# Hybrid decoder trunk: the chunk inverse in two halves, the K and R projections as one block

## What is computed

```python
def step(S, inp):
    r_t, w_t, k_t, v_t, kk_t, a_t = inp
    sa = jnp.einsum('bhvk,bhk->bhv', S, kk_t)
    S = (S * w_t[:, :, None, :] - sa[..., None] * (kk_t * a_t)[:, :, None, :]
         + v_t[..., None] * k_t[:, :, None, :])
    y = jnp.einsum('bhvk,bhk->bhv', S, r_t)
    return S, y
```

## Time and profile before

| | us |
|---|---|
| median of 3 runs | 1413.53 |
| the profiled execution's own time | 1413.33 |
| its span | 1411.5 |
| PE busy in the span | 1175.4 (83%) |
| DVE busy | 714.1 (51%) |
| ACT busy | 485.1 (34%) |
| POOL busy | 90.1 (6%) |

### The profile page before, as it was taken

One profiled execution on the slowest core, in us unless ns is written; L12 is line 12 of the kernel. 1 busy time (PEld: TensorE's weight loads), 2 busy tenths in 40 slices (PEclk: granted clock), 3 DMA queues, 4 the chain that ended last, 5 costly groups with the idle time before them and its releaser, 6 DMA issues. The chain is left out here.

```text
span 1411.5 us, 35169 instructions
## 1 busy us (share of the span) xinstructions
PE 1175.4 (83%) x15404; PEld 1055.4 (75%) x15404; DVE 714.1 (51%) x1101; ACT 485.1 (34%) x787; POOL 90.1 (6%) x145
## 2 busy tenths in 40 slices
PE   4868999999999967786999996159999999699953
PEld 1367888888888847556999996149998989699941
DVE  2236566566666534843333321855666666522226
ACT  0435353353454342333222221044444444322202
POOL 0002022022022101000000000000000000000000
PEclk9879999999999987657999998569999999899985
DMA  8231011101101006694332324112333223133221
GB/s 273 83 95 50 20 36 53 39 16 52 52 3 37 4 4 193 172 308 122 90 96 80 93 74 135 60 46 76 89 89 88 77 73 89 52 89 91 67 101 57
DMA packets 185347, 117.30 MB, mean 83 GB/s; under 512 B 6624, under 2 KB 177430, under 8 KB 184935
## 3 DMA queue, kind: packets, MB, share of 16 engines
q1 hardware_dynamic: 185233, 115.58, 27.9%
HBM read 108.40 MB, written 7.34 MB: 82 GB/s over the span
## 5 line engine op out<-in xcount | busy, mean ns | idle before, releaser
L199 PE MATMUL PJ<-Hh,Wh 128*128 128x260 f32 (+1 forms) x1088 | 245.0, 307 | 49.4 <-DVE Wl L1809 20.0
L199 PE MATMUL PJ<-Hh,Wl 128*128 128x260 f32 (+1 forms) x1088 | 223.9, 288 | 1.4 <-issue 1.4
L199 PE MATMUL PJ<-Hl,Wh 128*128 128x260 f32 (+1 forms) x1088 | 225.0, 289 | 0.0
L199 PEld LDWEIGHTS PJ<-Hh,Wh 128*128 128x128 f32 x1088 | 173.4, 194 | 68.4 <-issue 27.2
L199 PEld LDWEIGHTS PJ<-Hh,Wl 128*128 128x128 f32 x1088 | 173.3, 193 | 1.6 <-issue 1.6
L199 PEld LDWEIGHTS PJ<-Hl,Wh 128*128 128x128 f32 x1088 | 173.7, 194 | 0.0
L1809 DVE TENSOR_TENSOR Wl<-RAW,Wh 128x1024 fp32r<-128x1024 f32 (+1 forms) x68 | 80.8, 1194 | 101.0 <-ACT Wh L1749 96.3
L1749 ACT ACTIVATE Wh<-RAW 128x1024 fp32r<-128x1024 f32 (+1 forms) x68 | 70.1, 1036 | 111.5 <-PE PJ L199 103.8
L1503 DVE TENSOR_TENSOR Wl<-RAW,Wh 128x1024 fp32r<-128x1024 f32 (+1 forms) x40 | 44.7, 1119 | 112.3 <-ACT Wh L1465 111.6
L1829 DVE SCALAR_TENSOR_TENSOR ACC<-ACC,CP 128x512 f32<-128x512 f32 x88 | 66.1, 751 | 69.6 <-ACT ACC L1760 68.0
L199 PE MATMUL PJ<-SFh,Wh 128*128 128x260 f32 x352 | 71.9, 286 | 13.2 <-DVE Wl L1809 13.2
(11 more groups left out here) (318 smaller groups left out, 2274.0 us busy)
## 6 DMA issues: line engine op xcount, KB each, us to landing
RAW<-in_w_in_dram SPq DMA_DIRECT2D x46, 512.0 KB, 4.1
RAW<-in_ffn_up_dram SPq DMA_DIRECT2D x44, 512.0 KB, 3.7
RAW<-in_ada_w_dram SPq DMA_DIRECT2D x32, 512.0 KB, 6.0
RAW<-in_ffn_down_dram SPq DMA_DIRECT2D x16, 512.0 KB, 3.8
RAW<-in_ada_w_dram SPq DMA_DIRECT2D x2, 2048.0 KB, 10.6
ACC<-in_ada_w_dram SPq DMA_DIRECT2D x2, 2048.0 KB, 13.3
RAW<-in_w_branch_rwkv_dram SPq DMA_DIRECT2D x8, 512.0 KB, 3.8
RAW<-in_w_out_dram SPq DMA_DIRECT2D x8, 512.0 KB, 3.8
```

The source lines that it names most:

```text
L199: mm = pe.matmul(out[:, b, 0:nb[b]], w[:, slot, kw, :], x[:, kx, c0:c0 + nb[b]], start=first and w is Wh and x is xh, stop=last and w is Wl)
```

## The change

The order of the work in `slot(c)` and the place of its results in PSUM change; the products stay the same.

- Each level 1 to 5 is issued in two halves `f` (chunks 0 to 3, and 4 to 7): X, XI, TI and its eviction are half as large and twice as many, each half in two BB banks of its own. TT is one group again, into PJ[0], and one eviction.
- No `dense` inside the levels: `dense(2 * KT)`, the 16 k-steps of K and R, stands behind level 5, then `ss`, then W. The other 8 k-steps keep their places.
- `center(c - 1)` moves ahead of level 1, `variance(c - 1)` into level 1; values, the keys' transposes and keys x values go to levels 2, 3 and 4, each after X, through PJ[1].
- DVE's and ACT's preparation of tile `c + 1` moves behind the levels. `group_floor` moves from DVE to ACT. `roots` moves behind the eviction of W.
- On DVE `read_out` moves ahead of the first state's product, `unit_key` to the scan's step 1, `removal` to 2 to 4 and `group` to 5 to 7. On POOL `affine` and `samples` come after level 2's MO instead of level 1's.

```diff
@@ TensorE, slot(c)
                     mm.then_inc(S("mm_tt"), 1)
-                    for j in range(NJ):
-                        for h in range(2):
-                            mm = pe.matmul(B[3][HH[h], j * C:(j + 1) * C], ARI[HH[h], j ^ 1, 0, :], I2[HH[h], :], start=True, stop=True)
-                    mm.then_inc(S("t_in"), 1)
-
+                    if prv:
+                        center(c - 1)
...
+                    X0, TI0 = (2 * LEVELS - 1) * c, 2 * (LEVELS - 2) * c
                     for lv in range(1, LEVELS):
                         pe.wait_ge(S("mo"), (LEVELS - 1) * c + lv)
...
-                        for j in order:
-                            r, q = x_pos(lv, j)
-                            ti = j if lv == 1 else flat(x_pos(lv - 1, j))
-                            for h in range(2):
-                                mm = pe.matmul(B[r][b_at(lv, h, j), q * C:(q + 1) * C], MO[bp(h, j), lv % 2, j, :], TI[bp(h, j), ti, :],
-                                               start=True, stop=True)
-                        mm.then_inc(S("mm_x"), 1)
-                        dense(2)
...
+                        order = (0, 1, 2, 3) if lv % 2 else (0, 2, 1, 3)
+                        for f in range(2):
+                            if lv > 1:
+                                pe.wait_ge(S("ti"), TI0 + 2 * (lv - 2) + f + 1)
...
+                                    mm = pe.matmul(B[2 * f + r][b_at(lv, h, j), q * C:(q + 1) * C], MO[bp(h, j), lv % 2, j, :],
+                                                   TI[bp(h, j), j if lv == 1 else x_at(lv - 1, j), :], start=True, stop=True)
+                            mm.then_inc(S("mm_x"), 1)
+                        if lv == 1 and prv:
+                            variance(c - 1)
+                        if lv == 2:
+                            after(pe, "lnv", c)
+                            values()
+                        if lv == 3:
+                            keys_a()
+                        if lv == 4:
+                            new_values()
+                        pe.wait_ge(S("tt"), LEVELS * c + lv)
...
+                        for f in range(2):
+                            pe.wait_ge(S("xi"), X0 + 2 * lv + f)
+                            if lv < LEVELS - 1:
+                                ...
+                                mm.then_inc(S("mm_ti"), 1)
+                            ...
                         mm.then_inc(S("mm_tt"), 1)
-                        if lv == 1 and prv:
-                            center(c - 1, nxt)
-                        if lv == 2 and prv:
-                            variance(c - 1)
-                        if lv == 4 and nxt:
-                            ss(c + 1)
-                        dense(2 if lv == LEVELS - 1 else 1)
-
+
+                    dense(2 * KT)
+                    if nxt:
+                        ss(c + 1)
                     pe.wait_ge(S("tt"), LEVELS * (c + 1))
+                    pe.wait_ge(S("nv_ev"), c + 1)
@@ ScalarE
+                def group_floor(c):
+                    act.wait_ge(S("mm_gn"), 2 * c + 2)
+                    act.activation(YQ, PJ[1][:, 1, :], ACT.Identity, bias=CST[:, C_EPS + 1:C_EPS + 2], scale=1.0 / HD).then_inc(S("lnv"), 1)
...
+                    for lv in range(1, LEVELS - 1):
+                        for f in range(2):
+                            act.wait_ge(S("mm_ti"), TI0 + 2 * (lv - 1) + f + 1)
+                            act.activation(TI[:, 4 * f:4 * f + 4, :].rearrange("p (r q) t -> p r (q t)", r=2), BB[:, 2 * f:2 * f + 2, 128:256], ACT.Copy).then_inc(S("ti"), 1)
+                        if lv == 1 and prv:
+                            group_floor(c - 1)
+...
                     if nxt:
+                        split(num(c + 1, R_))
                         decays(c + 1)
                         split(num(c + 1, V_))
...
                 center(KT - 1)
+                group_floor(KT - 1)
                 roots(KT + 2, slice(TN, TN + T), ("lnv", KT))
@@ VectorE
+                    for lv in range(1, LEVELS):
+                        for f in range(2):
+                            dve.wait_ge(S("mm_x"), X0 + 2 * lv + f)
+                            dve.tensor_tensor(XI[:, 4 * f:4 * f + 4, :]..., BB[:, 2 * f:2 * f + 2, 0:128]..., I2..., ALU.add).then_inc(S("xi"), 1)
+                        dve.wait_ge(S("mm_tt"), LEVELS * c + lv + 1)
+                        dve.tensor_copy(by_type(TT), bank2(PJ[0], 4)).then_inc(S("tt"), 1)
                     if nxt:
+                        lo(num(c + 1, R_))
                         cumulate(c + 1)
+                        key_gain(c + 1)
+                        lo(num(c + 1, V_))
+                        shift(num(c + 1, K_), 1, XK, om(c + 1, K_))
+                        key(c + 1)
+                        if c + 2 < KT:
                             lo(num(c + 2, K_))
+                        norm_floor(c + 1)
...
+                    for j in range(1, NJ):
+                        dve.wait_ge(S("mm_s"), (NJ - 1) * c + j)
+                        dve.scalar_tensor_tensor(SS[:, j + 1, :], ...).then_inc(S("s"), 1)
+                        if j == 1 and nxt:
+                            unit_key(c + 1)
+                        if 2 <= j <= 4 and nxt:
+                            removal(c + 1, j - 2)
+                        if j >= 5 and prv:
+                            group(c - 1, j - 5)
```

More of the change, by code:

```diff
@@ L647, in slot @@
                     pe.wait_ge(S("tr_ev"), 4 * c + 2)
-                    for j in (0, 2, 1, 3, 4, 6, 5, 7):
-                        r, q = x_pos(1, j)
+                    for j in range(NJ):
+                        at = C * (j >> 1)
                         for h in range(2):
-                            mm = pe.matmul(B[r][b_at(1, h, j), q * C:(q + 1) * C], I2[bp(h, j), :], MO[bp(h, j), 0, j, :], start=True, stop=True)
+                            mm = pe.matmul(B[j & 1][HH[h], at:at + C], I2[bp(h, j), :], MO[bp(h, j), 0, j, :], start=True, stop=True)
@@ L652, in slot, with values @@
                     mm.then_inc(S("mm_tt"), 1)
-                    for j in range(NJ):
-                        for h in range(2):
-                            mm = pe.matmul(B[3][HH[h], j * C:(j + 1) * C], ARI[HH[h], j ^ 1, 0, :], I2[HH[h], :], start=True, stop=True)
-                    mm.then_inc(S("t_in"), 1)
+                    if prv:
+                        center(c - 1)
+                    def values():
+                        pe.wait_ge(S("xs"), num(c, V_) + 1)
+                        for j in range(NJ):
+                            at = C * (j >> 1)
+                            for h in range(2):
+                                mm = pe.matmul(PJ[1][kq(h, j), 1 - j % 2, at:at + C], VX[HH[h], j * C:(j + 1) * C], I2[HH[h], :], start=True, stop=True)
+                        mm.then_inc(S("t_in"), 1)
@@ new lines, in keys_a, with new_values @@
+                    def keys_a():
+                        pe.wait_ge(S("tr_ev"), 4 * c + 3)
+                        for j in (0, 1, 3, 2, 4, 5, 7, 6):
+                            at = C * (a_at(j) % 4)
+                            for h in range(2):
+                                mm = pe.matmul(PJ[1][b_at(LEVELS, h, j), pt(j), at:at + C], ARI[HH[h], j, 0, :], I2[HH[h], :], start=True, stop=True)
+                        mm.then_inc(S("t_in"), 1)
+                    def new_values():
+                        pe.wait_ge(S("tr_ev"), 4 * c + 4)
+                        for j in (0, 2, 1, 3, 4, 6, 5, 7):
+                            at = C * (2 * pt(j) + (j >> 2))
+                            for h in range(2):
+                                mm = pe.matmul(PJ[1][b_at(LEVELS, h, j), 1 - (j >> 1 & 1), at:at + C], KP[kq(h, j), j ^ 1, 0, :], VT[kq(h, j), j ^ 1, :],
+                                               start=True, stop=True)
+                        mm.then_inc(S("mm_nv"), 1)
@@ L691, in slot @@
[L691 to L705, removed]
@@ new lines, in slot @@
+                        for f in range(2):
+                            pe.wait_ge(S("xi"), X0 + 2 * lv + f)
+                            if lv < LEVELS - 1:
+                                for j in order:
+                                    j += 4 * f
+                                    r, q = x_pos(lv, j)
+                                    for h in range(2):
+                                        mm = pe.matmul(B[2 * f + r][bp(h, j), 128 + q * C:128 + (q + 1) * C], TT[b_at(lv, h, j), t_at(lv, j), :],
+                                                       XI[b_at(lv, h, j), x_at(lv, j), :], start=True, stop=True)
+                                mm.then_inc(S("mm_ti"), 1)
+                            for j in (0, 1, 3, 2):
+                                j += 4 * f
+                                at = C * (j >> 1)
+                                for h in range(2):
+                                    mm = pe.matmul(PJ[0][b_at(lv + 1, h, j), pt(j), at:at + C], XI[b_at(lv, h, j), x_at(lv, j), :],
```

(34 more changed lines are left out.)

191 lines of the change are left out of this document (84 added, 107 removed).

## The result

The changed kernel took 1435.44 us in the median of 4 runs (1434.08 to 1436.56). Its ratio to the kernel before is 1.0157, with a 95% interval of 1.0138 to 1.0177. It is 22 us slower, where 8.6 us faster was forecast. The profiled span grew by 23.0 us, from 1411.5 to 1434.5.

The account below looks back on a forecast made before the run. In slots with projections TensorE's own list was taken to set the time. Terms -14.0 - 4.45 + 7.8 + 0.85 + 1.2 = -8.6 us took the median of 1413.53 to 1405 us, range 1395 to 1421.

Parts of the forecast that it names:

- The levels in halves: Levels 1 to 5 issued in halves: period 2.35 us, set by DVE's evictions and the wait for TT; 2.5 us in levels 2 to 4.
- The term of -14.0: X of level 1 to W, slots 0 to 6: 24.8 us instead of 26.8, a gain of 2.0 us a slot.
- -4.45: Slot 7, which has no projections: W 12.85 us behind X of level 1 against 17.3, a gain of 4.45 us.
- Level 1: First level in halves, with `variance` put at 0.9 us: TT's second half starts 2.15 us behind X.
- Rival (a): Levels 2 to 5 of all slots exceed 2.5 us: gain gone from 2.75, 1421 us at 3.0; chance 0.14.
- Rival (c): TensorE's clock falls: first 2 us of each block's projections take 4, 14 us in all, 1419 us; chance 0.05.
- the slot's end: Last transposition waits as group step 2 moves behind scan step 7: +1.3 us in slots 1 to 6, +0.85 in slot 7.
- the table load at the tail: After slot 7 the root's table load can follow only ACT's scaling of the variance: +1.2 us.
- the k-steps' pace inside the block: Block behind level 5: 16 k-steps 11.7 us, in and out 0.3, `ss` with its change of operand kind 0.95.
- `center` costs nothing: Moved ahead of level 1, where TensorE waits for TT of level 0 anyway: no cost.

## Why the prediction was wrong

**The failed step is the period of the levels in "The levels in halves".** It took the chain TT copy, XI, TI, eviction, X as all that a level needs: 2.35 us, 2.5 with an extra group. The chain was right (2.53 and 2.40 in slot 1, halves of 0.415 and 0.383 us). What it left out is that a level with an extra group has 256 TensorE instructions, which at 2.5 us is 102 a microsecond, and these arrive at some 65: 3.7 to 4.0 us from stop to stop in slots 3 to 5. The term of -14.0 became +15.7, and -4.45 became -1.2. Adding many or few instructions at the same TensorE time shows this directly. In slots 0 to 6 the stretch missed its forecast by 29.7 us: 23.7 us are gaps put down to issue and about 1.5 the clock in slot 5. Level 1 was mis-sized besides: TT's second half starts 2.43 to 2.58 us behind X in slots 1 to 6, where 2.15 was forecast, some 2 us in all. The rest, about 2 us, is not assigned.

**The rows had a warning.** Level 4 of slot 7 ran 132 matmuls and 128 weight loads in 4.00 us, 65 a microsecond, and I read that row for the clock only. The head of slot 4 before has the same pace, and over 12 us the fastest stretch before is this one of slot 7 (windows of the kernel before):

```profile
331.00:338.40 7.40, 6.91 (x234) 5.79 (x236) 6.09 (x10) 3.75 (x9) 3.43 (x8) 1.00 0.61 166
...
486.20:498.20 12.00, 9.15 (x418) 7.81 (x418) 6.78 (x10) 4.45 (x8) 6.88 (x10) 1.00 0.01 4
```

470 in 7.40 us is 64 a microsecond, 836 in 12 us is 70; the halves asked for 102 in levels 2 to 4 and, with 1088 instructions in 11.85 us, 92 over all five. Over short stretches such a pace is possible: slot 1 of the changed kernel has 220 matmuls and 224 weight loads in the 4 us from 185.9, 111 a microsecond, before its first stop. The stretch that was rewritten ran at (622 + 618) / 26.8 = 46. The k-steps, 12 instructions in 0.73 us, kept it there: they covered not only evictions but the arrival of instructions. In the block behind the levels TensorE needs only 16 a microsecond.

**Rival (a)** named the place and the sign: at 3.0 us a level 1421 us. Its reasons, POOL's MO and the price of a half eviction, were wrong, and in slots 3 to 5 the levels were longer still. With 0.14 it had too small a chance, since the only pace looked at was slot 7's 3.00 us a level.

**Rival (c)** came true in part. Slot 5's and slot 7's dips cost about 1.5 and 1.9 us (33.6 against 32.0; 2.7 less the 0.85 of the slot's end). Slot 7's fall is not the change's alone: in the run with the square moved, whose slot 7 is the kernel before's, W to transposition took 14.3 us against 12.0. What decides when the clock falls stays open.

**Right:** the slot's end (+1.30 in six slots), its cause, the table load at the tail, the k-steps' pace inside the block (from 362.80, 12.8 us for 16 k-steps and ss, with TensorE busy throughout), and that `center` costs nothing in its new place. The cost of the slot's end was right as a wait; as a price it is not settled, since the run without it returned 5.6 us, not 8.5, with the clock differing in three slots.

**Open:** why slots 1, 2 and 6 get through two levels or more before the first stop and slots 3 to 5 do not. Where the blocks' boundaries fall in the levels differs from slot to slot, but no run moved them on purpose.

## What to carry to other kernels

Before taking big instructions out of a stretch of small ones, count the engine's instructions per microsecond that the new order asks for, and compare with the fastest pace that the trace has over some 10 us or more; here that was 65 to 70 on TensorE, while 4 us could hold 111. A gap put down to "issue" in the middle of a group, at a fixed count of instructions after the last such gap, is this wait. Long instructions between short ones cover it as they cover evictions, so a stretch that two waits hold back gains from removing one only until the other takes over.

## What was not expected of the hardware

- TensorE's instructions arrived in blocks, with stops 254 counted instructions apart and 3.7 to 4.0 us in slots 3 and 4 of the changed kernel (3.3 to 3.9 us in the run with 3584 more). The time is a round of three steps and not the DMA engines' load, which was 2%.
- A granted clock of 0.65 over 4 us in the middle of the stage, in one slot of the seven with projections. Slots 3 and 4, with the same kind of stops, had 1.00.
- The clock in one slot differs between executions of nearly the same order: slot 3 had 1.00 in the changed kernel and 0.62 at the start of its block in the run with the exchange on VectorE.
